# Two-block transformer kernel on one Trainium2 core: the lanes of the second block on a 128-point period, and 32x32 diagonal blocks inverted on GpSimd in place of 16x16

## What is computed

```python
def _rwkv7_scan(r, w, k, v, a_vec, b_vec):
    def step(S, inp):
        r_t, w_t, k_t, v_t, a_t, b_t = inp
        sa = jnp.einsum('bhij,bhj->bhi', S, a_t)
        S = S * w_t[:, :, None, :] + sa[..., None] * b_t[:, :, None, :] + v_t[..., None] * k_t[:, :, None, :]
        return S, jnp.einsum('bhij,bhj->bhi', S, r_t)

def _hgrn2_chunkwise(q, log_f, k, i):
    def step(S, inp):
        q_c, lf_c, k_c, i_c = inp
        b = jnp.cumsum(lf_c, axis=1)
        diff = b[:, :, None] - b[:, None, :]
        decay = jnp.where(causal, jnp.exp(jnp.where(causal, diff, 0.0)), 0.0)
        att = jnp.einsum('btshd,bshd->btsh', q_c[:, :, None] * decay, k_c)
        o_intra = jnp.einsum('btsh,bshv->bthv', att, i_c)
        o_inter = jnp.einsum('bthd,bhdv->bthv', q_c * jnp.exp(b), S)
        ...

y = jnp.einsum('btc,cd->btd', jnp.concatenate([o_rwkv, o_hgrn], axis=-1), w_out[l])
h = _layer_norm(ALPHA * h + y, ln_w[l], ln_b[l])
```

## Time and profile before

| what | value |
|---|---|
| median of 3 runs | 3040.19 us (3036.09 to 3040.61) |
| profiled execution, its own time | 3039.28 us |
| its span, first to last instruction | 3036.6 us |
| mean granted TensorE clock | 0.989 of 2.4 GHz |
| PE busy | 2954.9 us (97%) |
| DVE, ACT, POOL busy | 1682.6, 1254.5, 288.9 us |

### The profile page before, as it was taken

The page is one execution under the profiler, slowest core; times in us unless marked ns, Lnnn a source line. Parts: engine busy times, 40 slices in busy tenths (PEclk is TensorE's granted clock), DMA queues, the critical chain, the costliest instruction groups (busy, mean ns, idle before and its releaser), DMA issues.

```text
span 3036.6 us, 40030 instructions
## 1 busy us (share of the span) xinstructions
PE 2954.9 (97%) x15674; PEld 2377.9 (78%) x15674; DVE 1682.6 (55%) x3024; ACT 1254.5 (41%) x2206; POOL 288.9 (10%) x517
## 2 busy tenths in 40 slices
PE   9999999999999999999999999999999999999897
PEld 7878888787878887777778877787787877877786
DVE  6555555555453336566653365656666666564647
ACT  5444444434342335355443333434444343444412
POOL 0110101010000000000000002202022020212001
PEclk9999999999999999999999999999999999999999
DMA  4222222222234322222233322223222231224334
GB/s 170 77 84 84 84 77 84 82 82 81 84 118 147 110 91 70 77 77 70 70 130 132 119 86 82 84 65 92 76 73 92 64 100 59 89 79 153 129 131 156
DMA packets 86154, 289.16 MB, mean 95 GB/s; under 512 B 12096, under 2 KB 12864, under 8 KB 85712
## 3 DMA queue, kind: packets, MB, share of 16 engines
q1 hardware_dynamic: 69840, 243.79, 23.8%
q0 software_dynamic: 16128, 42.81, 4.6%
HBM read 261.26 MB, written 25.17 MB: 94 GB/s over the span
## 4 chain that ended last, share of the span: by engine, by line
PE 84%; DVE 7%; ACT 4%; issue 3%; DMA 1%; POOL 1%; DVEq 0%; SPq 0%; ACTq 0%; POOLq 0%
PE bank L281 16%; PE bank L283 15%; PE bank L282 15%; PE bank L285 7%; PE bank L287 7%; PE bank L286 7%; PE bank L1383 2%; PE bank L338 1%; PE bank L318 1%; ACT mc_split L564 1%; DVE mc_split L734 1%; PE bank L1290 1%; PE bank L467 1%; PE bank L480 1%; PE bank L1311 1%
## 5 line engine op out<-in xcount | busy, mean ns | idle before, releaser
L281 PE MATMUL bank<-ma_split,mc_split 128*128 128x512 f32 x2304 | 955.3, 415 | 12.1 <-DVE ma_split L893 7.1
L734 DVE TENSOR_TENSOR mc_split<-mc,mc_split 128x1024 fp32r<-128x1024 f32 x434 | 535.1, 1234 | 764.5 <-ACT mc_split L564 763.6
L283 PE MATMUL bank<-ma_split,mc_split 128*128 128x512 f32 x2304 | 905.4, 393 | 0.0
L282 PE MATMUL bank<-ma_split,mc_split 128*128 128x512 f32 x2304 | 902.8, 392 | 0.0
L564 ACT ACTIVATE mc_split<-mc 128x1024 fp32r<-128x1024 f32 x434 | 457.5, 1055 | 647.3 <-PE bank L285 345.2
L281 PEld LDWEIGHTS bank<-ma_split,mc_split 128*128 128x128 f32 x2304 | 435.7, 189 | 123.3 <-issue 49.2
L283 PEld LDWEIGHTS bank<-ma_split,mc_split 128*128 128x128 f32 x2304 | 434.4, 189 | 96.2
L282 PEld LDWEIGHTS bank<-ma_split,mc_split 128*128 128x128 f32 x2304 | 436.5, 189 | 78.6 <-issue 4.4
L285 PE MATMUL bank<-mc_split,ma_split 128*128 128x512 f32 x576 | 230.4, 400 | 5.0 <-DVE mb L1803 3.4
L287 PE MATMUL bank<-mc_split,ma_split 128*128 128x512 f32 x576 | 225.2, 391 | 0.0
L286 PE MATMUL bank<-mc_split,ma_split 128*128 128x512 f32 x576 | 224.7, 390 | 0.0
(11 more groups left out here) (363 smaller groups left out, 3639.9 us busy)
## 6 DMA issues: line engine op xcount, KB each, us to landing
mc<-in_w SPq DMA_DIRECT2D x434, 512.0 KB, 3.3
x<-mc POOLq DMA_DIRECT2D x8, 1024.0 KB, 5.0
y<-mb_split SPq DMA_DIRECT2D x28, 256.0 KB, 2.4
ma_split<-y POOLq DMA_DIRECT2D x28, 256.0 KB, 4.4
mb<-in_xt SPq DMA_DIRECT2D x8, 512.0 KB, 9.4
mc<-in_x POOLq DMA_DIRECT2D x4, 1024.0 KB, 5.6
mc<-x POOLq DMA_DIRECT2D x4, 1024.0 KB, 7.8
mats<-mc POOLq DMA_DIRECT2D x32, 128.0 KB, 2.2
```

Of the source, the lines that this page charges most:

```text
L281: mm = pe.matmul(banks[j][:], wh[:, c], act_hi[:, kt, :], start=(kt == 0), stop=False)
L282: pe.matmul(banks[j][:], wl[:, c], act_hi[:, kt, :], start=False, stop=False)
L283: last = pe.matmul(banks[j][:], wh[:, c], act_lo[:, kt, :], start=False, stop=(kt == KT - 1))
L734: dve.tensor_tensor(w_low[:, s % NR, :, :], w_raw[:, s % NR, :, :], w_high[:, s % NH, :, :].bitcast(F32), ALU.subtract).then_inc(w_lo, 1)
```

## The change

- `SUB` goes from 16 to 32 and `FIRST_LEVEL` from 4 to 5: GpSimd inverts 4 diagonal blocks of 32x32 a matrix, over 31 elimination steps instead of 15, on 128 partitions instead of 64. The diagonal blocks are loaded four times (one copy for each group of 32 partitions), and stored by four DMAs. The level-4 steps X, W and T go.
- The blocks are now rw 0, wa, hg 0, rw 1, hg 1, ..., rw 7, hg 7. Every unit and head has the same place in a period of 128 points: `G` at 37 to 46, `X` of the first level at 107 (at 110 in the last unit), the unit's end at 178 to 193. A head is spread over 117 points; the last two heads had rates of 2.3 and 2.0 points a step, now 4.5 and 4.0.
- The first output group takes its first 14 contraction tiles in one block of 7 slots, and the two tiles that hold the last unit and head in a one-slot block (`LATE`) behind the second group. The partial sum is kept in `xr[0]`.
- SP loads `x2` and the gains for the first two output groups; the POOL queue did. Ten of the loads of y (`y_loads`) stand ahead of the last unit's inversion in the POOL queue, and four within it.
- In a head, the attention diagonal is one matmul of `ones` with the product q*k (128x512) instead of four 128x128, and level 0 scales only q.

The core of the diff:

```diff
 LEVELS = 7
-SUB = 16
+SUB = 32
 SUBS = CH // SUB
-FIRST_LEVEL = 4
+FIRST_LEVEL = 5
+ROWS = 2 * NCH * SUBS * SUB // P
 MAT_STRIDE = SUBS * (SUB * CH + SUB)
 RANK = 64
...
 UNITS = 8
 OUT2 = RW0 + 2 * UNITS + 1
-BLOCKS = OUT2 + GROUPS
-SLOT0 = [8 * b if b <= WA else 8 * b - 6 for b in range(BLOCKS)]
+LATE = OUT2 + 2
+BLOCKS = OUT2 + GROUPS + 1
+SLOTS = [2 if b == WA else 7 if b == OUT2 else 1 if b == LATE else 16 if b == BLOCKS - 1 else 8 for b in range(BLOCKS)]
+SLOT0 = [sum(SLOTS[:b]) for b in range(BLOCKS)]
 
 TOTAL_SLOTS = SLOT0[-1] + 2 * BLOCK_SLOTS
-Y_ORDER = [*range(UNITS - 1), *range(UNITS, 2 * UNITS - 1), UNITS - 1, 2 * UNITS - 1]
+Y_ORDER = [*range(UNITS - 2), *range(UNITS, 2 * UNITS - 2), UNITS - 2, 2 * UNITS - 2, UNITS - 1, 2 * UNITS - 1]
 
 NR, NH, LEAD = 5, 3, 2
...
 
-            KIND = [("rw", 0), ("wa", 0), ("rw", 1)]
-            for i in range(UNITS - 2):
-                KIND += [("hg", i), ("rw", i + 2)]
-            KIND += [("hg", i) for i in (UNITS - 2, UNITS - 1)] + [("out", n) for n in range(GROUPS)]
+            KIND = [("rw", 0), ("wa", 0)]
+            for i in range(UNITS - 1):
+                KIND += [("hg", i), ("rw", i + 1)]
+            KIND += [("hg", UNITS - 1), ("out", 0), ("out", 1), ("late", 0), ("out", 2), ("out", 3)]
             assert RW0 + len(KIND) == BLOCKS and KIND[OUT2 - RW0] == ("out", 0)
...
 
             LANE0 = RW0 + 2
-            CHUNK_K = 24
+            STATE = 4 + 3 * (LEVELS - FIRST_LEVEL)
+            CHUNK_K = STATE + 3 * NCH - 1
             PART_B, CHUNKS = 8, 12
             END = CHUNKS + CHUNK_K
 
             def rw_at(u, k):
 
-                i = k - CHUNKS
-                late = 0 if u else 5
+                i, begin = k - CHUNKS, 128 * u
...
-                    return (128 * u - 54 if u else 7) + 2 * k
+                    return begin + 9 + 9 * k // 4
                 if k < CHUNKS:
-                    return 120 * u + 16 + late + 2 * (k - PART_B)
-                begin = 120 * u + 26 + late
+                    return begin + 28 + 2 * (k - PART_B)
                 if i < 4:
-                    return begin + 2 * i
-                if i < 13:
-                    return begin + 54 + 5 * (i - 4) // 2
+                    return begin + 37 + 3 * i
+                if u == UNITS - 1:
+                    return begin + (110 + 5 * (i - 4) // 2 if i < CHUNK_K else 152 + 3 * (i - CHUNK_K))
+                if i < STATE:
+                    return begin + 107 + 5 * (i - 4) // 2
                 if i < CHUNK_K:
-                    return begin + 77 + 5 * (i - 13) // 2
-                return begin + 105 + 3 * (i - CHUNK_K)
+                    return begin + (122 + 5 * (i - STATE) // 2 if i < STATE + 4 else 135 + 3 * (i - STATE - 4))
+                return begin + 178 + 3 * (i - CHUNK_K)
 
             def hg_at(h, m):
 
-                rate = {UNITS - 2: 23, UNITS - 1: 20}.get(h, 45)
-                return 64 * (BLOCK_OF["hg", h] + 1 - LANE0) + 1 + m * rate // 10
+                return 128 * h + 65 + m * (40 if h == UNITS - 1 else 45) // 10
 
             RW_K, HG_M = END + 6, 27
...
                     AT.setdefault(hg_at(u, m), ([], []))[1].append((u, m))
 
...
-                        to, frm = halves(to, lv)[1], halves(frm, lv)[1]
-                    for c in range(NCH):
-                        mm = pe.matmul(to[:, c], lhs[:, c * P:(c + 1) * P], frm[:, c], start=True, stop=True)
+                        pe.wait_ge(h_mix, MIXES * h + 2 * lv + 1)
+                        lhs = mix[lv % 2] if lv else hk
+                        to, frm = halves(four(D_BANK[:]), lv)[1], halves(four(mix[lv % 2]), lv)[1]
+                        for c in range(NCH):
+                            mm = pe.matmul(to[:, c], lhs[:, c * P:(c + 1) * P], frm[:, c], start=True, stop=True)
+                    else:
+                        pe.wait_ge(h_qk, h + 1)
+                        mm = pe.matmul(D_BANK[:], ones[:], hqk, start=True, stop=True)
                     mm.then_inc(d_done, 1)
                 if m == 17:
...
                 pool.wait_ge(a_out, 16 * NCH * (u + 1))
-                pool.dma_start(ub, blocks(a["mats"])).then_inc(ub_in, 16)
+                groups = [slice(2 * NCH * SUBS * r, 2 * NCH * SUBS * (r + 1)) for r in range(SUB // ROWS)]
+                for rows in groups:
+                    pool.dma_start(ub[rows, 0:SUB - 1, :], blocks(a["mats"])[:, 0:SUB - 1, :]).then_inc(ub_in, 16)
+                if u == UNITS - 1:
+                    y_loads(pool, range(10, 12))
                 if u:
-                    pool.wait_ge(yb_out, 16 * u)
-                n = (2 * SUB) * u
...
                 for k in range(SUB - 1):
-                    size = [2 * NCH * SUBS, k + 1, SUB - 1 - k]
+                    kept = k // len(groups) + 1
+                    size = [P, kept, SUB - 1 - k]
+                    pool.wait_ge(inv_step, n + 2 * k + 1)
+                    pool.tensor_tensor(yt[:, 0:kept, k + 1:SUB], yb[:, 0:kept, k:k + 1].broadcast_to(size),
+                                       ub[:, k:k + 1, k + 1:SUB].broadcast_to(size), ALU.mult).then_inc(inv_step, 1)
                     pool.wait_ge(inv_step, n + 2 * k + 2)
-                    pool.tensor_tensor(yt[:, 0:k + 1, k + 1:SUB], yb[:, 0:k + 1, k:k + 1].broadcast_to(size),
-                                       ub[:, k:k + 1, k + 1:SUB].broadcast_to(size), ALU.mult).then_inc(inv_step, 1)
-                    pool.wait_ge(inv_step, n + 2 * k + 3)
-                    pool.tensor_tensor(yb[:, 0:k + 1, k + 1:SUB], yb[:, 0:k + 1, k + 1:SUB], yt[:, 0:k + 1, k + 1:SUB],
+                    pool.tensor_tensor(yb[:, 0:kept, k + 1:SUB], yb[:, 0:kept, k + 1:SUB], yt[:, 0:kept, k + 1:SUB],
                                        ALU.add).then_inc(inv_step, 1)
-                pool.wait_ge(inv_step, n + 2 * SUB)
-                pool.dma_start(blocks(a["inv"]), yb).then_inc(yb_out, 16)
-                pool.wait_ge(yb_out, 16 * (u + 1))
+                pool.wait_ge(inv_step, n + 2 * SUB - 1)
+                for r, rows in enumerate(groups):
+                    pool.dma_start(blocks(a["inv"])[:, r::len(groups), :], yb[rows, :, :]).then_inc(yb_out, 16)
+                pool.wait_ge(yb_out, 16 * len(groups) * (u + 1))
                 c_wait(pool, "pe", u - 1, f"U{NCH - 1}")
                 pool.dma_start(xt, mats(a["inv"])).then_inc(xt_in, 16)
+                if u == UNITS - 1:
...
+                    y_loads(pool, range(12, 14))
                 pool.wait_ge(xt_in, 16 * (u + 1))
 
+            def x2_load(queue, n):
+
+                queue.dma_start(xr[n % 2], a["x2"].rearrange("(t p) n -> p t n", p=P)[:, :, n * N:(n + 1) * N]
+                               ).then_inc(x2_in[n], 16)
+                queue.dma_start(gb[n % 2], a["final_g"][:, n * N:(n + 1) * N].broadcast_to([P, N])).then_inc(x2_in[n], 16)
+
+            def y_loads(queue, which):
+
+                for i in which:
+                    kt = Y_ORDER[i]
+                    queue.wait_ge(w_free, SLOT0[OUT2 - 1] + i // 2 + 2)
+                    if kt < UNITS:
+                        queue.wait_ge(y_rw_st, 32 * (kt + 1))
+                    else:
+                        queue.wait_ge(y_h_st, 32 * (kt - UNITS + 1))
+                    queue.dma_start(h_hi[:, i, :], a["y2"][0, kt]).then_inc(y_in[i // 2], 16)
+                    queue.dma_start(h_lo[:, i, :], a["y2"][1, kt]).then_inc(y_in[i // 2], 16)
+
             def second_pool(pool):
-                x2_rows = a["x2"].rearrange("(t p) n -> p t n", p=P)
                 pool.wait_ge(m8_zeroed, 1)
                 pool.dma_start(a["inv"].rearrange("(p n) -> p n", p=P),
                                m8.rearrange("p q n -> p (q n)")[:, 0:2 * NCH * MAT_STRIDE // P]).then_inc(inv_zeroed, 16)
-                pool.wait_ge(inv_zeroed, 16)
-                for u in range(UNITS):
+                pool.wait_ge(x1_turned, 2 * KT)
+                pool.wait_ge(x1_sq, 2 * KT)
+                pool.dma_start(y0, a["eye"]).then_inc(inv_zeroed, 16)
+                pool.wait_ge(inv_zeroed, 32)
+                for u in range(UNITS - 1):
                     sub_inverses(pool, u)
-
-                for i, kt in enumerate(Y_ORDER[:KT - 2]):
-                    pool.wait_ge(w_free, SLOT0[OUT2 - 1] + i // 2 + 2)
-                    if kt < UNITS:
-                        pool.wait_ge(y_rw_st, 32 * (kt + 1))
-                    else:
-                        pool.wait_ge(y_h_st, 32 * (kt - UNITS + 1))
-                    pool.dma_start(h_hi[:, i, :], a["y2"][0, kt]).then_inc(y_in[i // 2], 16)
-                    pool.dma_start(h_lo[:, i, :], a["y2"][1, kt]).then_inc(y_in[i // 2], 16)
...
-                    if n >= 2:
-                        for t in range(TT):
-                            pool.wait_ge(bank_free[t], freed(OUT2 + n - 1, t))
-                    pool.dma_start(xr[n % 2], x2_rows[:, :, n * N:(n + 1) * N]).then_inc(x2_in[n % 2], 16)
```

(33 more changed lines are left out.)

120 lines of the change are left out of this document (63 added, 57 removed).

## The result

| | before | after |
|---|---|---|
| median | 3040.40 us (3036.09 to 3041.39, 4 runs) | 3106.53 us (3104.70 to 3107.55, 4 runs) |
| profiled execution, its own time | 3039.28 us | 3107.17 us |
| its span | 3036.6 us | 3105.4 us |
| mean granted clock | 0.989 | 0.979 |

The ratio is 1.022, with a 95% interval of 1.0202 to 1.0237. The change makes the kernel 66 us slower. The prediction was 3066 us, 26 us slower, with a range of 2970 to 3105. The direction was as forecast. The size was not, and the time lies 1.5 us above the range.

The account below looks back on a forecast made before the run. PE was taken as the bound. Span 3036.6 - 27 (work) - 55 (waits, slow clock) + 89 (X waits) + 20 (clock after them) = 3063.6 us, with 2.7 us around it 3066; range 2970 to 3105.

Parts of the forecast that it names:

- I give 55 of the 60 us back: Second block, PE: the new table's wider spacing removes 55 of 60 us of waits and slow clock.
- The other end of this term, 25 us: Second block, PE: only 25 us of waits and slow clock come back if the waits only move.
- Rival D in its second form: A with only 25 us given back elsewhere, 3096 us; both forms of D together had chance 0.09.
- A's upper end (3102): The forecast itself: PE waits 8 to 16 us at nearly every unit's first X; 16 gives 3102; A's chance 0.55.
- Work removed, 27 us: PE: dropping level 4's X, W and T steps saves 3.4 us a unit, 27 us over 8 units.
- The chain, 58 us, with a window of 46: G to X through GpSimd: xt ready after 58 us, PE at X after 46, so it waits 12 us a unit.
- rival C's case: The GpSimd chain fits wholly in PE's window and only the gains are left: 2957 us, chance 0.09.
- B's: GpSimd nearly undisturbed, xt ready at 47 to 53 us, PE waits 1 to 7 us: 2989 us, chance 0.27.
- the sum of the waits, 89 us: PE at X: 12 us in each of seven units and 5 us in the last, 89 us.
- The slow clock, 20 us: PE behind each X wait: the lower clock costs about 2.5 us in each of eight units, 20 us.
- The edits costed at nothing: Late block taken as 0 of a possible 0 to 3 us; single diagonal matmul worth nothing, 8.8 us against 8.7.

Follow-up runs that it names:

- experiment 1: The change with 16x16 blocks on GpSimd and level 4 back on TensorE (from point 99, last unit 102), the new table kept: 3028.29 us, ratio 0.9964.
- experiment 2: The change with only the first 11 of 31 elimination steps (inverses unfinished), all else issued as in the change: 3000.61 us, ratio 0.9873.
- Experiments 8 and 9: On experiment 1: head's turn (m = 17) two points later, 3016.57 us; or unit steps V, N, B, K at points 28, 31, 33, 35, 3024.17 us.
- experiment 5: The change with the chunk steps from X at points 113 to 153, evenly 2.5 apart, instead of from 107 with a gap: 3085.25 us, ratio 1.0162.

## Why the prediction was right and wrong

**The step that failed** is "I give 55 of the 60 us back". It took the idle time and the slow clock of before as something that the new table removes, since its steps stand further apart. Measured are 11 us, in experiment 1 (11.7 by experiment 2 with the predicted price of level 4; the two are not independent). They are mostly slow clock, of which the term had 13 us: of the 47.5 us idle only 2 to 3 came back. The named waits did go, but a table with a fixed period has its own collisions, and each comes in every period: 1.26 us at the head's turn seven times, 1.4 at N seven times, some 2.3 at the take seven times. The idle time without X was 47.6 us before and 49.0 after. The other end of this term, 25 us, was too high as well. With 11 in place of 55 the prediction's own sum is 3066 + 44 = 3110, and the measured time is 3106.5. Rival D in its second form (the chain as forecast, only 25 given back, 3096) named this cause, and had part of a chance of 0.09. By the number alone A's upper end (3102) is nearer, but with waits of 16 us at X that no unit had (7.3 to 13.5).

What could have shown the turn ahead is the table itself: the square root of k = 2 and the head's turn stand on one point. N stands two points behind V, but it did so before too, where it waited for V's copy in two units only; in unit 3 of the change that copy (2246.06) stands on ScalarE behind a slot's split (2245.11) and two operations that had waited 3.49 us for VectorE. Experiments 8 and 9 show these as causes: moving each one number by one or two points gave 12 and 4 us, and the gains add up. For the take the cause is open. Moving the unit's end to either side trades its wait for others. The later end costs 17 us, of which 10.9 are idle time (PE busy for 1109.2 us in the window against 1120.1); a mean clock of 0.98 there against 0.99 may hold the rest.

**Work removed, 27 us**: 27.7 measured, experiment 1 against 2.

**The chain, 58 us, with a window of 46.** From G to X are 59 to 62 us in units 0 to 6 (60.3 on average), and 66 in the last (55 predicted). The elimination's 62 x 0.54 = 33.3 was 34.1 in unit 3. The 2.6 cycles an element of the Trainium skill (GPSIMD Engine Reference, section 3.1) would make it 6.8 us, an estimate (with it xt would have been ready after some 32 us, which is rival C's case and not B's, where the prediction put it); the trace speaks against that as a price for chains of small dependent operations, since even the last ones, with 8 and 16 elements, start 0.29 to 0.33 us apart. The landing of the block loads was under-sized: the first operation starts 17.5 us behind G in unit 3 (2281.73 - 2264.23), where the prediction's terms make 13.0 (10.5 from G to the first operation in unit 5 before, by the earlier trace rows, and 2.5 for the four loads). What follows the elimination was over-sized: 9.2 us in every unit, where 9.1 in unit 5 before and the 2.6 of the four stores make 11.7. So the chain is 60.3 us and not 58. The window was under-sized by about as much. PE's own time from G to X is 49.2 us in the change and 48.9 in experiment 2, where X does not wait, in part because the take's wait lies in it (2.3 us in unit 3 of experiment 2; 3.4 in the change, with two smaller waits). In the last unit both errors are larger, 66 for 55 and 59 for 50. The errors cancelled, so that the sum of the waits, 89 us, came out as 85.1 is in part luck.

**The slow clock, 20 us**: 16 by the difference to experiment 2.

**Rivals B and C** needed an elimination under 26 us; no unit had one (33.4 to 34.3). Experiment 2 is C made by hand. Even with a free chain the time is 3000.6, not 2957, again by the 44 us of the failed term.

**The edits costed at nothing** (the late block, the single diagonal matmul, the queue's moves) lie within the 11 us and were not measured apart. One of them shows in the trace of the change. In the last unit the first operation of the elimination starts 22.7 us behind G, where units 0 to 6 have 17.2 on average: the last store of the matrices, behind loads of y on the same queue, lands after 5.48 us of waiting where unit 3 has 3.05, and two more pairs of loads of y (issued 2870.45 to 2872.64, after 7.12 us in which POOL stood) come ahead of the elimination. That lies in the last unit's wait of 7.3 us.

The change thus consists of +78 us for the inversion and -11 us for the rest. The inversion saves PE 27.7 us and costs it 105.9. Its waits of 11.1 us a unit are as long as 16 points of products. But experiment 5 shows that such room brings less than its length: 6 points took 2.7 us off a wait and gave 21 us in all, and the steps behind X had to go closer together for it. At that rate some 25 points would be needed, an estimate.

## What to carry to other kernels

Work moved from the bounding engine to a slow one pays only if the bounding engine then waits less for the chain through the slow one, with its DMAs, than the work had cost (here 27.7 us saved and 105.9 lost); price that chain operation by operation from rows taken beside the same neighbours, and charge the lower clock after each wait too. Never credit a new order of issue with the waits of the old one: list, for the new order, each place where two lanes meet on a bank or an engine, price it as if it comes in every period, and take the credit only for what is left. After the change, compare the idle time without the wait that you expected; if it has not fallen, move one number at a time.

## What the runs showed of the hardware

The four loads of the diagonal blocks (124 KB each) landed later than the one 64 KB load of before: median 6.8 us from issue to landing against 4.1. The last load was as before (4.6 and 4.8), though in experiments 1 and 2, where X does not wait, it took 5.9. The page's DMA issues:

```profile
mc<-inv POOLq DMA_DIRECT2D x8, 512.0 KB, 4.6
...
mc<-mats POOLq DMA_DIRECT2D x32, 124.0 KB, 6.8
```

Small dependent GpSimd operations started 0.33 us apart with 24 and with 16 elements and 0.29 apart with 8, of which 0.21 to 0.26 are their busy time. Four of the last five rows of POOL's elimination in unit 3 of the change, in its timeline:

```profile
2314.33 0.26 POOL L2059 TENSOR_TENSOR mc<-mc 128x24 f32<-128x24 f32 x1
2314.66 0.24 POOL L2056 TENSOR_TENSOR mc<-mc 128x16 f32<-128x16 f32 x1
2314.99 0.25 POOL L2059 TENSOR_TENSOR mc<-mc 128x16 f32<-128x16 f32 x1
2315.31 0.21 POOL L2056 TENSOR_TENSOR mc<-mc 128x8 f32<-128x8 f32 x1
```

ScalarE's load of an activation table took 1.28 us, and the operation behind it started 0.02 us after its end. The Trainium skill (ScalarE: Activation LUTs, "What ACT_TABLE_LOAD costs") gives about 1.28 us for the load and about 1.38 us more for a drain. The trace has the first figure and no idle time for the second: behind 99 of the 148 loads of the change, the next operation starts at most 0.02 us after the load's end.
